# Cached attention pages loaded two rows to a partition, and a batch's eight heads scored in one pass

## The reference, cut to what matters

```
suffix = lax.cumsum(lf, axis=1, reverse=True) - lf
k_all = jnp.concatenate([k_past, k_new], axis=1)          # past: 8 pages x 128 rows, through page_table
v_all = jnp.concatenate([v_past, v_new], axis=1)
...
s = jnp.einsum('bqhd,bkhd->bhqk', q, k_all) * scale
s = s + fq[..., None] - fk[:, :, None, :]                 # fk: -suffix of the log forget gates, then the new ones
p = jax.nn.softmax(jnp.where(mask, s, -jnp.inf), axis=-1)
out = jnp.einsum('bhqk,bkhd->bqhd', p, v_all)
```

## Time and profile before

| what | value |
| --- | --- |
| median of 3 runs | 2067.64 us (2061.04 to 2072.47) |
| profiled execution, its own time | 2069.19 us |
| its span, first to last instruction | 2067.6 us |
| mean granted TensorE clock | 0.942 |
| PE busy, share of the span | 1680.2 us, 81% |
| DVE busy | 686.3 us, 33% |
| ACT busy | 310.4 us, 15% |
| bytes moved by DMA | 674.12 MB, mean 326 GB/s |
| key and value pieces | 128 issues each, 256 KB a piece |

### The profile page before, as it was taken

The page is one execution under the profiler, slowest core; times in us unless marked ns, Lnnn a source line. Parts: engine busy times, 40 slices in busy tenths (PEclk is TensorE's granted clock), DMA queues, the critical chain, the costliest instruction groups (busy, mean ns, idle before and its releaser), DMA issues. The chain is left out here.

```text
span 2067.6 us, 33965 instructions
## 1 busy us (share of the span) xinstructions
PE 1680.2 (81%) x13033; PEld 1016.8 (49%) x13034; DVE 686.3 (33%) x1821; ACT 310.4 (15%) x665; POOL 354.5 (17%) x453
## 2 busy tenths in 40 slices
PE   5897989597789887775699999887687899987765
PEld 3455664354455454442355666664344555544432
DVE  0211235611422331221621256546412333331126
ACT  0121201111111111000002244331011011110110
POOL 3000100132221221221001122100122222221210
PEclk8999999699999999998799999998799999999997
DMA  9479883799999999994832589996599999999966
GB/s 329 148 286 335 313 317 115 309 419 424 423 385 385 418 421 410 398 397 159 321 110 96 192 275 328 325 354 220 210 424 422 408 420 408 421 419 408 409 256 224
DMA packets 132059, 674.12 MB, mean 326 GB/s; under 512 B 28111, under 2 KB 40527, under 8 KB 91620
## 3 DMA queue, kind: packets, MB, share of 16 engines
q1 hardware_dynamic: 84880, 570.20, 69.8%
q10 hardware_dynamic: 21604, 55.96, 8.1%
q0 software_dynamic: 25456, 46.27, 6.2%
HBM read 651.03 MB, written 46.94 MB: 338 GB/s over the span
## 5 line engine op out<-in xcount | busy, mean ns | idle before, releaser
L2346 PE MATMUL bank<-ring,work 128*64 128x256 f32 x4128 | 486.7, 389 | 107.8 <-DMA ring<-in_exp_w 104.4
L2346 PEld LDWEIGHTS bank<-ring,work 128*64 128x64 f32 x4128 | 329.0, 140 | 302.3 <-issue 118.3
L2358 PE MATMUL bank<-ring,work 128*64 128x512 f32 x1032 | 251.5, 605 | 62.5 <-DVE work L1782 60.4
L813 POOL DMA_INDIRECT work<-u_d,work x128 | 129.4, 1011 | 772.5 <-DVE work L1750 422.8
L2074 PE MATMUL bank<-ring,uT 128*128 128x512 f32 (+1 forms) x896 | 256.6, 502 | 6.4 <-DVE u L1499 4.2
L1750 DVE COPY work<-work 128x1 int32<-128x1 int32 (+1 forms) x128 | 19.3, 153 | 657.3 <-ACT work L1198 656.5
L2074 PEld LDWEIGHTS bank<-ring,uT 128*128 128x128 f32 (+1 forms) x896 | 118.9, 169 | 135.0 <-issue 114.3
L820 POOL DMA_INDIRECT pair_d<-work x128 | 133.2, 1040 | 114.0 <-issue 75.6
L2358 PEld LDWEIGHTS bank<-ring,work 128*64 128x64 f32 x1032 | 73.9, 136 | 150.4 <-issue 147.2
L1192 ACT COPY work<-bank 128x512 f32<-128x512 f32 x128 | 75.1, 587 | 366.8 <-PE bank L2358 356.8
L1198 ACT ACTIVATE work<-bank 128x128 f32<-128x128 f32 x128 | 35.5, 278 | 531.5 <-PE bank L2346 531.5
(11 more groups left out here) (361 smaller groups left out, 1698.6 us busy)
## 6 DMA issues: line engine op xcount, KB each, us to landing
ring<-in_exp_w SPq DMA_DIRECT2D x128, 2048.0 KB
ring<-in_exp_w SPq DMA_DIRECT2D x128, 1024.0 KB
ring<-in_ada_w SPq DMA_DIRECT2D x24, 2048.0 KB, 11.9
ring<-in_cache_k SPq DMA_DIRECT2D x128, 256.0 KB, 6.3
ring<-in_cache_v SPq DMA_DIRECT2D x128, 256.0 KB, 7.0
ring<-in_gla_w_in SPq DMA_DIRECT2D x6, 2048.0 KB, 14.0
ring<-in_kv_w_mod SPq DMA_DIRECT2D x4, 2048.0 KB, 10.0
work<-pair_d ACTq DMA_DIRECT2D x4, 2048.0 KB, 9.6
```

What stands on the lines that cost most here:

```text
L813: pool.indirect_dma_start(out=xg[:, s, :], out_offset=None, in_=u_d, in_offset=bass.IndirectOffsetOnAxis(ap=xi[:, s:s + 1], axis=0), bound ...
L2346: ins = mm(psum[s][64 * c:64 * c + 64, 0:2 * P].rearrange("p (a n) -> p a n", a=2), xT[:, s, j * P + 64 * half:j * P + 64 * half + 64], gu ...
L2358: ins = mm(psum[3 + s][64 * c:64 * c + 64, :], hT[:, s, 64 * f:64 * f + 64], w[:, f, c * 512:(c + 1) * 512], start=(f == 0), stop=(f == 1) ...
```

## The change

Four things change together.

- **Loads.** A page (128 rows of all 8 heads, 512 KB) is now one load. Two neighbouring rows go to one partition, 8 KB in one run, so a page fills 64 partitions: even pages partitions 0 to 63, odd pages 64 to 127. A pair of pages shares a ring unit. A "chunk" j is then 128 keys on 128 partitions (64 from each page of a pair), for all eight heads. Key and value loads are issued in another order, and the page's number is read just ahead of each load.
- **Steps.** One loop over 8 batches takes the place of the 16 groups. `turn_keys(b, j)` turns eight heads (heads 0 to 3 into bank 0, 4 to 7 into bank 1), `chunk_scores` scores eight heads, into banks 2 and 3 for the first four and 4 and 5 for the others. The probabilities' transposes now use banks 0 and 1 in turn with the keys; ACT copies the first half of them, DVE the second. A table (`TURN_AT`) counts these turns. The second half's scores have a buffer of their own in ring unit 8.
- **Order.** PE, ACT and DVE have new orders, below.
- **Biases.** ACT writes the suffix sums in the new order of the keys, with two strided copies in place of one.

```diff
-            def load_pages(b, first=False):
-                ...
-                    for j in range(PAGES):
-                        if not first:
-                            sp.wait_ge(kt_full, b * 16 + (8 * half + j - 15))
-                        rows = W["cache_k"][ds(page[j], 1)].rearrange("o r h d -> (o r) (h d)")
-                        sp.dma_start(key_page(half, j), rows[:, half * 512:(half + 1) * 512])\
-                          .then_inc(sem(f"k_landed{half}{j}"), 16)
...
+            def load_chunks(cache, unit, b, pair, landed):
+                for i in range(2):
+                    page = sp.value_load(pages[0:1, ds(b * PAGES + (2 * pair + i), 1)], min_val=0,
+                                         max_val=cache.shape[0] - 1)
+                    sp.dma_start(ring[64 * i:64 * i + 64, unit + pair, :],
+                                 cache[ds(page, 1)].rearrange("o (m r) h d -> (o m) (r h d)", r=2)).then_inc(landed, 16)
...
+            with sp.Fori(2, DB) as b:
+                for pair in range(2):
+                    sp.wait_ge(s_full, b * 8 + (2 * pair - 6))
+                    load_keys(b, pair)
+                sp.wait_ge(fo_full, b * 2 - 2)
+                load_values(b - 1)
+                for pair in range(2, 4):
+                    sp.wait_ge(s_full, b * 8 + (2 * pair - 6))
+                    load_keys(b, pair)
+            sp.wait_ge(fo_full, GROUPS - 2)
+            load_values(DB - 1)
             for j in range(2):
                 load_linear(("fox_wo", j), W["fox_w_o"], j)
...
+            def turn_keys(b, j):
+                if j % 2 == 0:
+                    pe.wait_ge(sem(f"k_landed{j // 2}"), 32 * (b + 1))
+                n = TURN_AT[("keys", b, j)]
+                for s in range(2):
+                    if n:
+                        pe.wait_ge(sem(("kt_act", "kt_dve")[s]), n)
+                    for i in range(4):
+                        ins = pe.transpose(psum[s][:, i * P:(i + 1) * P],
+                                           key_chunk(j)[:, (4 * s + i) * P:(4 * s + i + 1) * P], ident[:, :])
+                    ins.then_inc(turn_full[s], 1)
...
+            def values(b, s):
+                n = TURN_AT[("probs", b, s)] + 1
+                pe.wait_ge(sem("v_landed"), 128 * (b + 1))
...
+            pe.wait_ge(sem("sc_ready"), GROUPS)
             wait(pe, "o_prompt_done", GROUPS)
+            units = [weights_landed(pe, ("fox_wo", 0))]
             product(("fox_wo", 0, 0), 0, units[0])
-            turn_probs(GROUPS - 1)
+            turn_probs(DB - 1, 0)
+            values(DB - 1, 0)
+            turn_probs(DB - 1, 1)
+            values(DB - 1, 1)
```

More of the change, by code:

```diff
@@ L154, with fox_turns @@
 GROUPS = 2 * DB
+def fox_turns():
+    steps = []
+    for b in range(DB):
+        for j in range(PAGES):
+            steps.append(("keys", b, j))
+            if b and j in (2, 4):
+                steps.append(("probs", b - 1, j // 4))
+    steps += [("probs", DB - 1, s) for s in range(2)]
+    return {step: n for n, step in enumerate(steps)}
+TURN_AT = fox_turns()
+TURNS = len(TURN_AT)
 INPUTS = ["x_prompt", "x_sample", "c_prompt", "c_sample", "state_gla", "cache_k", "cache_v", "cache_logf",
@@ L1335, in _, with turned_keys, exponents, turned_probs @@
                 act.wait_ge(sem(f"kv_out{n}"), 32)
[L1337 to L1352, removed]
+            def turned_keys(b, j):
+                act.wait_ge(turn_full[0], TURN_AT[("keys", b, j)] + 1)
+                if 8 * b + j >= 2:
+                    act.wait_ge(s_full, 8 * b + j - 1)
+                act.copy(kt_sb[:, 2 * (j % 2), :], psum[0][:, :]).then_inc(sem("kt_act"), 1)
+            def exponents(b, s):
+                wait(act, "max_ready", 2 * b + s + 1)
+                act.activation(sc[s], sc[s], ACT.Exp, bias=stat[:, 16 + 2 * s:17 + 2 * s],
+                               accum_out=stat[:, 20 + s:21 + s]).then_inc(signal("exp_ready"), 1)
+            def turned_probs(b, s):
+                act.wait_ge(turn_full[0], TURN_AT[("probs", b, s)] + 1)
+                act.copy(pT[:, 0:4, :].rearrange("p a b -> p (a b)"), psum[0][:, :]).then_inc(sem("kt_act"), 1)
             def prompt_exponents(g):
@@ L2002, in old_scores @@
[L2002 to L2009, removed]
-                    .then_inc(sem("sc_ready"), 1)
+                dve.wait_ge(s_full, 8 * b + 4)
@@ L2038, in _ @@
+            for half in range(2):
+                turned_probs(DB - 1, half)
+                group_out(DB - 1, half)
+            out_turned(DB - 1)
             residual(2, "fox_wo", 4)
@@ new lines, in chunk_scores @@
+            def chunk_scores(b, j):
+                n = TURN_AT[("keys", b, j)] + 1
+                pe.wait_ge(sem("kt_act"), n)
+                pe.wait_ge(sem("kt_dve"), n)
+                if j == 0:
+                    wait(pe, "kn_ready", b + 1)
+                    if b:
+                        wait(pe, "sc_half", 2 * b)
+                if j == 4 and b:
+                    pe.wait_ge(sem("sc_ready"), 2 * b)
+                for s in range(2):
+                    for i in range(4):
+                        ins = mm(psum[2 + 2 * s + j // 4][32 * i:32 * i + 32, (j % 4) * P:(j % 4 + 1) * P],
+                                 qz[:, s, i, :], kt_sb[:, 2 * (j % 2) + s, i * P:(i + 1) * P], start=True, stop=True,
+                                 tile_position=(0, 32 * i), skip_group_check=True)
+                ins.then_inc(s_full, 1)
```

393 lines of the change are left out of this document (209 added, 184 removed).

## The result

The changed kernel took 2173.49 us (median of 4 runs, 2151.51 to 2184.35) beside 2068.2 for the kernel before. It is slower: 1.0477 times as long, 95% interval 1.0427 to 1.0526. This ratio is of means (2166.2 to 2067.5) and leaves the longest run out as disturbed, and the only profile is of that run (2184.35 us, span 2182.7). It stands 115.2 us above the profiled run of before (2069.19), 8 to 33 more than the other three do, so a part of what it shows may be its own.

What follows compares the result with a forecast made beforehand. It took PE and its DVE partners to bound the old page stage, pages almost, and half-partition transfers the changed one: 2069.2 + 81 (pages at 215 GB/s) + 5 (end of stage) = 2155 us, range 2080 to 2180.

Steps and rivals of the forecast that it cites:

- The rate: Page stage: loads to alternating halves of the partitions were taken to move 215 GB/s, so 62.9 MB need 292.6 us.
- ends of 196 and 425: Bounds for the page rate in GB/s: mean of the 64-partition profile rows, and the 128-partition rows.
- the tenth added to 196: Page loads: a load's last pieces overlap the next load's first in the other half, raising 196 GB/s to 215.
- The first output product: Page stage's end: PE's first product with the output weights starts at 1465.6 instead of 1384.5, +81 us.
- 62.9 MB must come after 1166: Page stage: 67.1 MB of pages less batch 0's keys of 4.2 MB remain to load, taking 292.6 us.
- the first rival: Page stage: halves load together at 425 GB/s, PE's new DVE waits slow it, 2095 us; chance 0.27 for 2080 to 2125.
- End of the stage: Behind the first output product, two groups of probabilities and values stand instead of one: about +5 us until the residual.
- PE's waits on DVE ... all lie inside this: Page stage: a batch needs 39 us of transfer, PE with its new waits some 29, so they add nothing to +81.
- the sign that I named: Page stage's waits: PE's value products wait longest, for values' pages, then the key transposes for keys.
- Its two new waits: Page stage at full rate: PE waits for DVE's copy at batch starts, +23 us, and the second prompt norm, +7.
- The granted clock: Page stage: a drop would make the prediction wrong, as PE then needs up to twice its time.
- PE and its DVE partners bound the stage, pages almost do: Kernel before, page stage: PE has some 23.2 us of work per 27 us batch; pages cost 5 to 12 us.

Runs made afterwards that it cites:

- e8: Changed kernel with each batch's eight value loads ordered four to the lower half of the partitions, then four to the upper, instead of in turn: 2183.91 us.
- e3: Changed kernel with each page's 64 runs of 8 KB sent to every second partition, biases in the matching order: 2109.73 us.
- e6: Changed kernel, half loads kept; ACT makes early key copies, second prompt norm goes earlier, first output weights load before last values: 2157.39 us.
- e1: Changed kernel with each page loaded to all 128 partitions in 4 KB runs, biases in ordinary key order: 2108.6 us; run again, 1.0251 times the kernel before.
- e11: Kernel before with the prompt's norm moved ahead of DVE's copy of the sixth page's turned keys: 2059.55 us beside 2064.33.
- e10: e1 plus twenty idle PE products per batch, placed where PE waits for DVE at the batch's start: 2104.66 us.
- e2: Kernel before with each 128-row piece loaded by two loads, partitions 0 to 63 and 64 to 127: 2232.99 us.

## Why the prediction was right, point by point

Forecast 2155 (2080 to 2180), slower at 0.85; measured 2173.49, 18 more. The mechanism held; the terms that missed were mostly too small.

**The rate: right.** I took 215 GB/s between ends of 196 and 425. The full stretches show 222, the window of the whole stage 209. That the choice fell so near is in part luck: the tenth added to 196 for loads that overlap in two halves isn't shown by any run, for e8, with four value loads to one half in a row, still has 217. That the target, one half of the partitions, is the cause is shown by e3, where the same 64 partitions' worth of bytes in the same runs went to every second partition and no page was waited for. The Trainium skill, "SBUF — State Buffer", section "Can I just issue two DMAs to hit both halves?", has 6% for two loads in flight, one to each half, by which I had estimated 208; the full stretch, 222, is 13% above 196, and the 209 includes times when the engines weren't full. The same page of the Trainium skill, section "Door 1: The DMA port swizzle (why `[64,N]` ≈ `[32,N]`)", says that partitions 0 to 63 reach only half of the memory's 16 ports, and that the lowest two bits of the partition number don't choose the port. By that every second partition reaches them all, and e3 agrees (280 GB/s at a share of 0.81, no wait for pages).

**The first output product: 1465.6 forecast, 1490.55 in the profile.** The mechanism held and the term "62.9 MB must come after 1166" was too small. The DMA page of the changed kernel from 1166 to 1490 us:

```profile
DMA packets 12558, 69.27 MB, mean 214 GB/s; under 512 B 3800, under 2 KB 3800, under 8 KB 4680
...
q1 hardware_dynamic: 9782, 65.64, 89.0%
```

69.27 MB moved, not 62.9 and 2.1 for the output weights. The other 4.3 MB are POOL's biases and new values (2.1), ACT's loads (1.1), instructions (0.5) and the first 0.6 of the second half of the output weights. I could have counted them, for the kernel before moves 67.09 MB from 1166 to 1384. At 222 GB/s they are 19 us; the pages at 222 instead of 215 give 9 back; the output weights at 222 instead of 420 cost 4.5 more; I had 2 for landing. 69.27 / 0.222 = 312 us, and in the other 12 of the 324 us the engines moved less. 20 x (222 - 131) / 222 = 8 of them are the hole from 1450 to 1470, and nearly 5 lie ahead of the first load, which SP issued at 1171.0 instead of 1165.9 (3 GB/s from 1166 to 1171). So the second thing that the step missed is that loads don't run back to back to the end: the last values wait for the buffer. I had that mechanism in the first rival (+7), and left it out of the sum where transfers bound. The three other runs, of 2151.51 to 2176.05 us, have no trace, so how much of the 25 us they share isn't known.

**End of the stage: +5 forecast, 9.1 measured.** Right in kind, short by 4.

**"PE's waits on DVE ... all lie inside this": nearly, or wholly.** e6 has 0.4 points less than the changed kernel, inside the noise, of the 1.7 that the same edits gave at full rate. But the sign that I named, PE's value products waiting longest, did not come: the norm (32.2) and the copies (19.5) hold PE longer than values (18.2) and keys (12.9), and only when e6 takes DVE's waits away do the values lead (48.8). PE was busy 71% of the stage, not some 60%. What I didn't have at all is the way back from the transfers to DVE: with the engines full the biases land late (8.6 us in the median, e1 4.2), DVE waits for them (11.3 us), and the norm's wait becomes 32.2 instead of e1's 20.0.

**The first rival, priced at 2095, was run as e1: 2108.6.** That is 45 above the kernel before beside it, where I had 26. Its two new waits were sized well: 23 forecast and 22.6 measured at the batches' starts; for the norm 14.0 + 7 = 21, and 20.0. Short were the output weights (0.94 + 7, measured 12.0), and the end (+2; in e1 2100.41 - 1408.21 = 692.2 us behind the first product, 7.5 more than before). The clock wasn't in the sum: 0.88 instead of 0.98.

**The granted clock** did drop, which I had named as what would make the forecast wrong. It did not make it wrong, since beside the transfers PE had time: it was busy 216.17 of 304 us.

**What bounds the kernel before.** "PE and its DVE partners bound the stage, pages almost do": e11 shows how nearly, 12.3 us of one turned into 6.1 of the other.

## What to carry to other kernels

Before making a transfer's runs longer, look at which partitions it writes: one half of them took a third of the rate away (323 to 222 GB/s at a full DMA share, although the runs were longer; in rows 3, whose runs are equal, 421 to 193), and every second one did not. When a kernel's transfer and its engines are close to even, price each end on its own, and count all bytes that cross the stage, the small ones too. And ask of a buffer that now serves two uses when it comes free: the loads behind it start only then.

## What the runs showed of the hardware

- The granted clock fell behind waits of PE. In e1 it was 0.50, the lower of its two levels (1.2 GHz), from 1276 to 1282 us, behind a wait of 3.54 us, and 1.00 (2.4 GHz) from 1284 to 1290. Eight transposes took 1.97 us behind the wait and 1.09 later, and 1.09 behind the idle products that filled it in e10. The stage's clock went from 0.98 to 0.88.
- 64 neighbouring partitions and 64 that are spread over all 128 are different targets: 222 GB/s at a DMA share of 1.02, with waits for pages, against 280 at 0.81 with none (e3).
- SP's issuing can bound a stage: 0.67 us a load in e2, 196 GB/s with loads of 128 KB.
